# Contracting the first sixteen FFN units with unscaled activations, behind a chunked load of x

## What is computed

```
ada = silu(c) @ w_ada + b_ada                      # shift, scale, gate for three sub-layers
n = rms_norm(h, g_ffn1) * (1 + scale) + shift      # sub-layer 1, h = x
h = h + 0.5 * gate * (silu(n @ w1_h) * (n @ w1_u)) @ w1_out
n = rms_norm(h, g_mix) * (1 + scale) + shift       # sub-layer 2
h = h + gate * (gate_a * conv_branch + gate_b * pool_branch) @ w_out
n = rms_norm(h, g_ffn2) * (1 + scale) + shift      # sub-layer 3, an FFN like the first
h = h + 0.5 * gate * (silu(n @ w2_h) * (n @ w2_u)) @ w2_out
return rms_norm(h, g_final)
```

## Time and profile before

| | us |
|---|---|
| median of the runs | 2600.87 (2597.87 and 2666.51 the others) |
| the profiled execution | 2596.2 |
| its span, slowest core | 2594.6 |
| spans of the eight cores | 2586.4 to 2594.6 |
| PE busy in the span | 2499.8 |

### The profile page before, as it was taken

The page is one execution under the profiler, slowest core; times in us unless marked ns, Lnnn a source line. Parts: engine busy times, 40 slices in busy tenths (PEclk is TensorE's granted clock), DMA queues, the critical chain, the costliest instruction groups (busy, mean ns, idle before and its releaser), DMA issues.

```text
span 2594.6 us, 38158 instructions; the slowest of 8 cores (2586.4 to 2594.6 us)
## 1 busy us (share of the span) xinstructions
PE 2499.8 (96%) x14726; PEld 1405.4 (54%) x14726; DVE 1023.2 (39%) x1487; ACT 429.3 (17%) x772; POOL 336.9 (13%) x605
## 2 busy tenths in 40 slices
PE   1999999999999999999999999999999999999997
PEld 0566666666666666677544444444444444444445
DVE  5467555444454546646832224610021100211026
ACT  3422000100000012523511111510000000000013
POOL 1220111111111110000111100000000000000034
PEclk9999999999999999999999999999999999999999
DMA  9999999899998984843385452454444445444435
GB/s 232 159 165 197 193 171 154 148 159 159 162 154 139 166 153 99 183 89 70 68 188 94 77 108 47 82 98 80 71 80 79 73 74 82 75 73 81 68 63 167
DMA packets 103888, 310.05 MB, mean 119 GB/s; under 512 B 11808, under 2 KB 26528, under 8 KB 103584
## 3 DMA queue, kind: packets, MB, share of 16 engines
q0 software_dynamic: 79024, 260.12, 60.9%
q1 hardware_dynamic: 24688, 47.50, 5.6%
HBM read 546.09 MB, written 16.78 MB: 217 GB/s over the span
## 4 chain that ended last, share of the span: by engine, by line
PE 91%; DMA 5%; ACT 1%; DVE 1%; issue 1%; POOL 0%; DVEq 0%; SPq 0%; ACTq 0%; POOLq 0%
PE ps L275 91%; DMA ring<-w_head 2%; DMA ring<-w_ada 1%; ACT nT L285 1%; DMA hT<-xT 1%; DMA ring<-w_out 1%; DVE U L289 1%; DVE rs L306 0%; DVE hT L300 0%; ACT L285 0%; POOL ring L322 0%; ACT rs L285 0%; DVE rs L289 0%; SPq L337 0%; ACTq L1107 0%
## 5 line engine op out<-in xcount | busy, mean ns | idle before, releaser
L275 PE MATMUL ps<-nT,ring 128*128 128x352 bf16 (+3 forms) x9344 | 1650.3, 339 | 15.0 <-DMA ring<-w_head 8.2
L275 PEld LDWEIGHTS ps<-nT,ring 128*128 128x128 bf16 x9344 | 914.0, 98 | 737.9 <-issue 22.5
L275 PE MATMUL ps<-U,ring 128*128 128x352 bf16 (+3 forms) x4480 | 794.7, 339 | 3.1 <-DMA ring<-w_out 3.1
L275 PEld LDWEIGHTS ps<-U,ring 128*128 128x128 bf16 x4480 | 435.9, 98 | 355.9 <-issue 5.0
L285 ACT ACTIVATE tmp<-ps 128x512 f32<-128x512 f32 (+1 forms) x268 | 142.7, 535 | 1708.8 <-PE ps L275 1678.4
L289 DVE TENSOR_TENSOR U<-tmp,ps 128x352 bf16<-128x352 f32 (+1 forms) x190 | 113.1, 598 | 769.0 <-PE ps L275 759.1
L300 DVE SCALAR_TENSOR_TENSOR hT<-ps,ghT,hT 128x352 f32<-128x352 f32 (+3 forms) x288 | 182.8, 636 | 355.7 <-PE ps L275 355.7
L322 POOL DMA_DIRECT2D ring<-w_in x212 | 112.5, 532 | 1189.8 <-PE ps L275 1175.4
L385 DVE SCALAR_TENSOR_TENSOR ring<-ring,rs 128x2048 bf16<-128x2048 bf16 x112 | 253.0, 2286 | 13.6 <-DMA ring<-w_adaD 13.6
L322 POOL DMA_DIRECT2D ring<-w_out x118 | 62.8, 533 | 507.0 <-PE ps L275 498.0
L285 ACT ACTIVATE nT<-hT 128x512 bf16<-128x512 f32 (+4 forms) x138 | 79.1, 582 | 183.7 <-DVE hT L300 174.0
(11 more groups left out here) (67 smaller groups left out, 592.3 us busy)
## 6 DMA issues: line engine op xcount, KB each, us to landing
ring<-w_in POOLq DMA_DIRECT2D x212, 512.0 KB, 6.6
ring<-w_adaD POOLq DMA_DIRECT2D x112, 512.0 KB, 9.9
ring<-w_out POOLq DMA_DIRECT2D x80, 512.0 KB, 5.5
hT<-xT SPq DMA_DIRECT2D x8, 2112.0 KB, 23.6
ring<-w_ada POOLq DMA_DIRECT2D x32, 512.0 KB, 18.5
ring<-w_out POOLq DMA_DIRECT2D x38, 384.0 KB, 6.1
hscr<-hT SPq DMA_DIRECT2D x16, 512.0 KB, 12.9
hT<-hscr SPq DMA_DIRECT2D x16, 512.0 KB, 13.2
```

The lines of the kernel that those rows point to most:

```text
L275: e.matmul(o, l, r, start=st, stop=sp, skip_group_check=sk),
```

## The change

- `NHEAD` goes from 10 to 12, with a new `HEAD_ORDER` and cuts of the contraction that depend on the unit.
- x comes chunk by chunk through four staging chunks of `hT` (`x_load`), each next load behind the `x_mod` of the chunk that it replaces. The fills no longer wait for x.
- `x_mod` no longer has the root or the shift: `nT` is x times (scale and gain), and a column 1056 of `nT` holds the shift, so the last block of each matmul group has 353 columns and gives, beside the sums, the constant term of each output column (`bias_col`).
- The sum of squares gathers in `rs`; the root (`x_root`) is taken behind `a31`, ahead of the first last part.
- A unit's end is `finish`, for each block of 352: h times root on **POOL**, Silu with bias on ACT, u times root on DVE, and a `scalar_tensor_tensor` on DVE (add bias, multiply). Two finishes are placed behind each last part from `u1.3` on; fourteen of the 36 remain and go into the units 12 to 15.
- Units 12 to 15 are `raw_unit`: like the others but with the root and bias in their eviction.
- `nT` is then rewritten with the normed operand by `rms_apply(0, ...)`, chunk 0 ahead of the first d loop and the others one for each d.
- x is reloaded chunk by chunk as parked sums are released; `cbc` is loaded behind the head instead of at the start; more ticks fall among units 16 to 31, fewer ahead of the first d loop.

Core of the diff:

```diff
-NHEAD = 10
-KCUTS = ((0, 4), (4, 7), (7, 11), (11, 16))
+NHEAD = 12
+CUTS_A = ((0, 4), (4, 8), (8, 12), (12, 16))
+CUTS_B = ((0, 3), (3, 7), (7, 11), (11, 16))
+CUTS_C = ((0, 6), (6, 12), (12, 16))
+KCUTS = [CUTS_A] * 1 + [CUTS_B] * 7 + [CUTS_C] * 4
 HEAD_ORDER = (
+    "a0 a1 a2 a3 a4 a5 u1.0 u3.0 u5.0 u4.0 a6 a7 u6.0 a8 "
+    "a9 u0.0 a10 u2.0 u7.0 a11 a12 u8.0 a13 u11.0 a14 u1.1 u10.0 u2.1 "
+    "u6.1 a15 a16 u9.0 a17 u5.1 a18 u4.1 u3.1 a19 a20 u7.1 a21 u0.1 "
+    "u7.2 u3.2 u4.2 u1.2 a22 a23 u5.2 u6.2 u9.1 u2.2 a24 u10.1 u0.2 a25 "
+    "u8.1 a26 a27 a28 a29 u11.1 a30 a31 u0.3 u1.3 u2.3 u3.3 u4.3 u5.3 "
+    "u6.3 u7.3 u8.2 u9.2 u10.2 u11.2 "
...
-                first_rd = [Bh.r(11)] if not slot_used else []
...
-                        if q0 == 0 or q % 2 == 0 and q0 == 32 or q % 4 == 0 and q0 == 16:
+                        if q0 == 0 or q % 2 == 0 or q % 8 in (1, 7) and q0 == 16:
                             tick()
...
+                if s == 0 and q0 == 0:
+                    run_late(0)
+                    rms_apply(0, 0, 0, T)
                 if q1 < NH:
                     for d in range(KC):
                         tick()
+                        if s == 0 and q0 == 0 and d + 1 < KC:
+                            rms_apply(0, d + 1, 0, T)
...
+            def finish(u, x, y):
+                ...
+                op_tt(h, h, rs[:, x:y], ALU.mult, [hr, Brs.r(0, x, y)], [hr], eng="pool")
+                op_act(tmp[:, ti, 0:w], h, AF.Silu, [hr, bias_r(u, 0)], [Btmp.r(ti, 0, w)], bias=bias_ap(u, 0))
+                op_tt(g, g, rs[:, x:y], ALU.mult, [gr, Brs.r(0, x, y)], [gr])
+
+                def close():
+                    op_stt(Bp.ap3[:, u, x:y], g, bias_ap(u, 1), tmp[:, ti, 0:w], ALU.add, ALU.mult,
+                           [gr, bias_r(u, 1), Btmp.r(ti, 0, w)], [Bp.r(u, x, y)])
+                    if y == T and u >= 6:
+                        x_reload(2 * (u - 6))
+                        x_reload(2 * (u - 6) + 1)
+                return close
...
+                if last and not rooted:
+                    x_root()
+                    rooted = True
...
+                if last:
+                    fins += [(u, x, y) for (x, y) in TB3]
+                    if u > 0:
+                        emit_finish()
+                        emit_finish()
...
+        def raw_unit(q, sh, su):
+            bks = pair_mm(sh, su, RAW_BLKS, False)
+            ...
+                op_tt(tmp[:, t1, 0:w], psum[bh][:, 0:w], rs[:, x:y], ALU.mult, [psr(bh), Brs.r(0, x, y)], [Btmp.r(t1, 0, w)])
+                op_act(tmp[:, t1, 0:w], tmp[:, t1, 0:w], AF.Silu, [Btmp.r(t1, 0, w), bias_r(q, 0)], [Btmp.r(t1, 0, w)],
+                       bias=bias_ap(q, 0))
+                op_tt(tmp[:, t2, 0:w], psum[bu][:, 0:w], rs[:, x:y], ALU.mult, [psr(bu), Brs.r(0, x, y)], [Btmp.r(t2, 0, w)])
+                ...
+                for f in more_fins * (2 if x == 704 else 1):
+                    f()
```

More of the change, by code:

```diff
@@ L335, in build_nc, with stage, x_load @@
         S.add("sp", lambda e: e.dma_start(out=pp[:], in_=ppd), writes=[Bpp.r(0)], dma="pp")
[L336 to L340, removed]
+        xtv = xT.rearrange("(k p) t -> p k t", p=P)
+        NST = 4
+        def stage(kc):
+            return KC - NST + kc % NST
+        def x_load(kc):
+            S.add("sp", lambda e: e.dma_start(out=hT[:, stage(kc), :], in_=xtv[:, kc, :]),
+                  writes=[Bh.r(stage(kc))], dma=("x", kc % NST))
+        for kc in range(NST):
+            x_load(kc)
         tmpflat = tmp[:].rearrange("p a b -> p (a b)")
@@ new lines, in bias_ap, with bias_col @@
+        def bias_ap(u, hu):
+            return bcol[:, 2 * u + hu:2 * u + hu + 1]
+        def bias_col(u, hu, bk, w, first):
+            if first == "act":
+                op_act(bias_ap(u, hu), psum[bk][:, w:w + 1], AF.Copy, [psr(bk)], [bias_r(u, hu)])
+            elif first:
+                op_copy(bias_ap(u, hu), psum[bk][:, w:w + 1], [psr(bk)], [bias_r(u, hu)])
+            else:
+                op_tt(bias_ap(u, hu), bias_ap(u, hu), psum[bk][:, w:w + 1], ALU.add, [psr(bk), bias_r(u, hu)], [bias_r(u, hu)])
@@ new lines, in build_nc, with run_late, x_reload, x_square @@
+        late = []
+        def run_late(keep):
+            while len(late) > keep:
+                late.pop(0)()
+        def x_reload(c):
+            S.add("sp", lambda e: e.dma_start(out=hT[:, c, :], in_=xtv[:, c, :]), writes=[Bh.r(c)], dma=("xr", c))
+        def ffn1_head():
+            def x_square(kc):
+                o, r = (rs[:], Brs.r(0)) if kc == 0 else (tmpflat[:, 0:T], Btmp.rr(0, 3))
+                op_act(o, hT[:, stage(kc), :], AF.Square, [Bh.r(stage(kc))], [r])
+                if kc:
+                    op_tt(rs[:], rs[:], tmpflat[:, 0:T], ALU.add, [Brs.r(0), Btmp.rr(0, 3)], [Brs.r(0)])
+            def x_mod(kc):
+                op_act(nT[:, kc, 0:T], hT[:, stage(kc), :], AF.Identity, [Bh.r(stage(kc)), Bgs.r(0, kc, kc + 1)], [Bn.r(kc, 0, T)],
+                       scale=gsT[:, kc:kc + 1])
+                op_copy(nT[:, kc, T:T + 1], adaT[:, kc:kc + 1], [Bada.r(0, kc, kc + 1)], [Bn.r(kc, T, T + 1)])
+            def x_root():
+                for (x, y) in TB3:
+                    bk = new_bank()
+                    op_mm(psum[bk][:, 0:y - x], ones32D[:], rs[:, x:y], True, True,
+                          reads=[("ones32D", 0, 1), Brs.r(0, x, y)], writes=[psr(bk)])
+                    rms_root(bk, x, y)
+            def finish(u, x, y):
+                w = y - x
+                ti = tctr[0] % 4
+                tctr[0] += 1
+                ph, pu = park(u, 0), park(u, 1)
+                h, hr, g, gr = ph.ap3[:, 0, x:y], ph.r(0, x, y), pu.ap3[:, 0, x:y], pu.r(0, x, y)
+                op_tt(h, h, rs[:, x:y], ALU.mult, [hr, Brs.r(0, x, y)], [hr], eng="pool")
[8 more added lines that the diff above has]
+                return close
+            def emit_finish():
+                if fins:
+                    u, x, y = fins.pop(0)
+                    late.append(finish(u, x, y))
+                    run_late(1)
+            fins = []
+            x_square(0)
+            x_square(1)
+            rooted = False
@@ L963, in ffn1_head @@
-            for i in range(0, KC, 4):
-                x_reload(i, i + 4, i)
+                        if y == T:
+                            bias_col(u, hu, bk, w, "act" if p == 0 else False)
+                if last:
[3 more added lines that the diff above has]
+                        emit_finish()
+            nbanks[0] = 8
+            cbuf = hT[:, KC - 4:KC - 2, :].rearrange("p a b -> p (a b)")[:, 0:D]
+            S.add("sp", lambda e: e.dma_start(out=cbuf, in_=cbc), writes=[Bh.rr(KC - 4, KC - 2)], dma="cb")
```

122 lines of the change are left out of this document (64 added, 58 removed), and 6 rows, old and new, of the table HEAD_ORDER.

## The result

| | before | after |
|---|---|---|
| median of the runs, us | 2599.37 | 2619.93 |
| lowest, highest | 2596.56, 2666.51 | 2619.41, 2620.64 |
| span of the slowest core, profiled execution | 2594.6 | 2618.2 |

The ratio is 1.0087, with a 95% interval of 1.0074 to 1.0099. Executions like that of 2666.51 us, in which cores get a lower clock and take longer, are left out of every ratio. The forecast was 2602 with 2618 as its upper end, so the kernel after is 2 us outside the range, on the slow side.

A forecast was written before the change was run, and what follows sets the result against it. DMA was taken to bound everything up to the first d loop at 326.5. 19 us saved in bytes and 22 given back by idle DMA made +4 on 2596.2, 2600.2; with half the scatter, 2602, range 2584 to 2618.

The forecast's parts named there:

- Up to a31: Head through a31: 60.4 MB at the earlier rate of 0.321 put a31's contraction at 197 us, against 188.4 before.
- The two bounds of the text: For the time of a31: 195.6 us by DMA bytes and 197.5 us by PE's own work.
- From a31 to the root: Behind a31: root matmuls of 3.86 us now on the path, reciprocals done at 208, PE stalling some 3 us.
- A last part costs DVE 5.5: Last parts: 4.8 us of DVE work plus 0.7 for contention with POOL, against 4.5 on PE; bounds 4.8 and 7.0.
- POOL's queue holds the fills: Last parts: fills wait behind the finishes' multiplies on POOL, unit 12's until 246 us; the cost thought to decide.
- Rival 1: Fills not held up much; d loop bound by bytes at 305 or PE at 316, gain 10, time 2588; chance 0.27.
- From there to the d loop: From unit 12's release at 246: 28.6 MB at 338 GB/s take 84.5 us, so the d loop starts at 330.5.
- all three engines meet: At the d loop's start: DMA ready at 330.5, PE at 326, DVE near 330.
- Behind it: From the first d loop on: rms_apply hidden, extra ticks in units 16 to 31 cost zero, bounds 0 and 5 us.
- rival 3: Extra ticks make units 16 to 31 DMA bound while the head gains nothing; 2608; chance 0.05.
- Rival 2: DVE and POOL block each other fully: part costs 7.0, unit 12 released at 255, d loop at 340; 2613 to 2618; chance 0.23.

The follow-up runs named there:

- e5: The kernel after with each part of w1_head packed contiguously in HBM, same bytes and order; ratio to the kernel before 1.0029.
- e11: The kernel before with w1_head packed contiguously, nothing else; ratio to the kernel before 0.9971.
- e4: The kernel after without the loads of x chunks 4 to 15 (6.5 MB), stale x used instead; ratio to the kernel before 1.0011.
- e12: The kernel after with w1_head packed contiguously and without the loads of x chunks 4 to 15; ratio to the kernel before 1.0008.
- e3: The kernel after with the root taken behind chunk 13, ahead of a31; spans 2611.8 to 2616.7 us on cores 4 to 7, no ratio given.
- e1: The kernel after with the finish's h multiply by the root on DVE instead of POOL; ratio to the kernel before 1.0097.
- e2: The kernel after with fills issued up to nine items ahead, as far as unit 14, multiplies still on POOL; ratio to the kernel before 1.0137.
- e8: The kernel after with the first nine w_adaD items still fetched but DVE's contraction of them left out; ratio to the kernel before 1.0072.
- e7: The kernel after with the nine ticks of units 13 to 15 moved behind the first d loop; ratio to the kernel before 1.0049.
- e9: The kernel after with the edits of e1, e3 and e7 and one finish behind each last part (two at u1); ratio to the kernel before 1.0011.
- e13: e9 with two finishes behind each last part again, as in the kernel after; ratio to the kernel before 1.0066.

## Why the prediction was wrong, step by step

The forecast started from +4 us; 23.6 were measured between the spans. Of the 19.6 missed, 11.1 lie ahead of a31 (its contraction at 208.1 against 197), 4.8 between a31 and the d loop (138.3 against 133.5), and 3.6 behind the start of the loop. The first is the step that failed.

**Up to a31: wrong, in one term.** The bytes were right, and so was the form of the sum. The rate was not: it was carried over from the earlier trace rows of the kernel before, 0.321 MB/us, where the kernel after has 0.307. (60.4 + 1.6) / 0.307 + 2.5 is 204.5. With e5's 0.329 the same formula gives 191.0, measured 190.7; with e11's 0.326 and the 59.5 MB of the kernel before it gives 185.0, measured 183.5. (With the mean rate of all cores, 0.312, it gives 201.2, where a31 ends at 205.6 on the mean: there the rate is 5 to 6 us of the miss and not 9.) Four us are left, 204.5 to 208.5. In that last stretch DMA is no longer full (0.66) and PE is short too: the granted clock was 0.83 from 188 to 208, and after waits of 1.17, 1.81 and 1.32 us the 36 matmuls at 200.60 took 7.27 us, where full-clock groups of 36 in the head took 5.54. From u0.1 (142.9, predicted 138.5) through a31 PE took 65.8 us, where I had 59 at full clock. The two bounds of the text, 195.6 by DMA and 197.5 by PE, both moved, and the range had no case for either.

Why the rate fell is shown in part. That the layout of `w1_head` takes part is shown by e5, at 13 to 18 us of a31. In the kernel before (e11) the same packing brings less, some 8 us by the ratio. It does not need x streaming beside it: without x, from 40 to 100 us, e4 reads 305 GB/s and e12, packed, 331 (two chips, but that is more than chips differ by here). So the streamed x is not what makes the pitched rows cost more in the kernel after. The order and the sizes of the parts are left (parts of six chunks are new), and no run changes them alone. How far apart the 16 engines end their share of one fill (median, 50 to 190 us, by the core) is 10 to 15 us in the kernel after, 6 to 9 in the kernel before, 4 to 6 in e5 and 6 to 8 in e4. So the spread narrows without x although the rate does not rise. The wait for a slot ends with the last engine, so a wide spread keeps ring slots waiting as well; what that costs is not shown. The Trainium skill (DMA: Bandwidth & Descriptors, Latency and other measured facts) reports copies between HBM tensors slowed by large power-of-two row pitches, and packing contiguously as a cure, with figures for pitches from 512 KiB up. The runs here agree with the cure at a pitch of 16 KB, for 7% of the rate on core 3 (307 to 329 GB/s), 5% on the mean.

**From a31 to the root: right.** The fill of u2.3 was due 14 us behind a31 and went out at 221.46, 13.4 behind. The stall showed as 4.83 us. Taking the root out of this stretch (e3) shortened it by 4.4 us, and the end by nothing, since ahead of a31 it costs as much.

**A last part costs DVE 5.5: right within 0.2, with the contention in it under-priced.** The pace is 5.45 in e1, and 5.7 on core 7 of the kernel after (one start of a finish to the next, 242.91 and 248.62). The groups of DVE by shape in the kernel after, 208 to 279 us (busy, mean ns):

```profile
L296 DVE TENSOR_TENSOR U<-ps,U 128x352 f32<-128x352 f32 x36 | 16.7, 510 | 2.2 <-PE ps L282 2.2
L296 DVE TENSOR_TENSOR U<-U,rs 128x352 f32<-128x352 f32 x18 | 16.0, 891 | 0.0
L307 DVE SCALAR_TENSOR_TENSOR U<-U,bcol,tmp 128x352 bf16<-128x352 f32 x18 | 11.7, 650 | 0.0
```

and in e1, core 0, 203 to 275 us, where no multiply runs on POOL:

```profile
L296 DVE TENSOR_TENSOR U<-U,rs 128x352 f32<-128x352 f32 x36 | 17.0, 513 | 0.0
...
L307 DVE SCALAR_TENSOR_TENSOR U<-U,bcol,tmp 128x352 bf16<-128x352 f32 x18 | 10.3, 574 | 0.9 <-ACT tmp L292 0.9
```

The multiply with two SBUF inputs takes 891 ns beside POOL's and 513 without them, the `scalar_tensor_tensor` 650 and 574. That is 0.38 on each of two multiplies in a part, and 0.08 on the two others: 0.9 instead of my 0.7. An own multiply of DVE costs 0.43, so two on DVE would cost 0.87. Moving them to POOL therefore gained DVE nothing, which is why e1 keeps the pace.

**POOL's queue holds the fills: right as a fact, wrong as the cost that decides.** The first fill of `w_in` was due 49 us behind a31 and came 50.2 behind (258.34), with DMA at 0.55 in between. But e1 and e2 removed the hold and gained nothing. The slots were not free either: a ring of ten that frees one slot for each 5.5 us part gives DMA a half load in any case. Rival 1, built on the absence of that hold (305 by bytes), falls by the same runs. I had named one holder of the fills and had not asked who was next.

**From there to the d loop: right.** 84.5 us by bytes, 88.1 measured. e8 and e7 confirm that bytes bind there, not DVE. That all three engines meet held only in part. By the mean span of the cores at 0.987 or more, e1, e2, e3 and e8, each of which relieves one engine or one queue, moved the end by 1 us at most, but e7, which takes bytes and DVE work out together, by 11, and e9 by 24. What e9 adds to e7 is nearly all the one finish (e13).

**Behind it: the 0 is right for units 16 to 31 and wrong for the loop.** No `ring` wait in units 16 to 31, by a PE busy for all of the 229 us; rival 3 falls. The loop lost 3.4 us, which the text had not priced, around a late `w_out`: waits of 0.17 and 2.35 us in it, and 48 matmuls in 9.62 us behind the wait of 7.56, at a granted clock of 0.76, where the next 48 took 7.32. In the kernel before, its first 80 ran slow as well (13.77 us). e7, with the bytes gone, runs the loop in 114.4.

**Rival 2** (2613 to 2618) came nearest to the time, but not by its mechanism: parts cost 5.7, not 7.0, and the release of unit 12 came where the forecast had it, counted from a31.

## What to carry to other kernels

A rate read from the stretch before holds for its access pattern, so when a change alters the queues, the parts and the order of a transfer-bound stretch, price that stretch once more at a rate some per cent lower, and give it a case of its own in the range: here 4% of rate was 9 us on the slowest core. Where several engines are within a few per cent of each other, an edit for one of them can show nothing (e1, e2, e3 and e8), so combine edits before a cause is dismissed, and then take them back one by one to see which of them paid. A fill that stands behind a compute instruction costs only what its slot would have allowed otherwise: look for the second holder before blaming the first.

## What the runs showed of the hardware

**The lock of the shared port can outlast one instruction.** DVE beside a burst of ten POOL multiplies in e2, core 7 (start, duration):

```profile
271.01 6.94 DVE L296 TENSOR_TENSOR hT<-hT,rs 128x352 f32<-128x352 f32 x1
...
278.37 0.51 DVE L296 TENSOR_TENSOR hT<-hT,rs 128x352 f32<-128x352 f32 x1
```

and POOL, same kernel and core:

```profile
268.68 8.89 POOL L296 TENSOR_TENSOR hT<-hT,rs 128x352 f32<-128x352 f32 x10
```

DVE's operation ends 0.4 us after the burst (277.95 and 277.57), after 6.94 us instead of 0.51; cores 0 and 6 show the same. The Trainium skill (SBUF — State Buffer, Terms), quoted in the prediction, has the pair held "for the full instruction"; the row is longer than one POOL multiply (0.89) by six to seven more, so back-to-back POOL instructions did not let DVE in between. In the kernel after the bursts among the last parts are mostly of one or two, and the multiplies beside them took at most 1.83 us (cores 0, 3 and 7); a burst of four at 289.49 on core 7 held one for 4.02.

**Small sizes.** The POOL multiply of 352 columns in place took 0.94 us, or 0.89 in a burst, against the 1.2 estimated from the earlier trace rows. A tick whose result feeds two one-column operations took DVE 2.77 us from start to start (298.83 to 301.60 on core 7), not the 2.3 of its long operation: the rest is dependent one-column work.
